# Experts' weights of a two-layer diffusion backbone in transfers of 2 MB, each filling two neighbouring slots of the weight ring

## The reference, cut to what matters

```python
def _ec_moe(h, router, w_gate, w_up, w_down):          # 16 experts, weights 1024 x 1024, float32
    cap = CAPACITY_FACTOR * n // N_EXPERTS             # 64 latent rows, 32 context rows
    aff = softmax(h @ router)
    g, idx = top_k(swapaxes(aff, 1, 2), cap)
    xs = h[bidx, idx]
    a, u = einsum(xs, w_gate), einsum(xs, w_up)
    y = einsum(silu(a) * u, w_down) * g
    return zeros_like(h).at[bidx, idx].add(y)
```

## Time and profile before

| | us |
|---|---|
| median of the runs | 2219.13 |
| the profiled execution, its time | 2219.71 |
| its span, first to last instruction | 2217.9 |
| PE busy (matmuls) | 1863.0 (84%) |
| VectorE, ScalarE, POOL busy | 569.7, 344.6, 265.2 |
| ring's queue (q1): 65952 packets, 480.28 MB | 54.0% of 16 engines' span |
| POOL's queue (q0): 17488 packets, 48.51 MB | 7.6% of 16 engines' span |
| mean granted TensorE clock | 0.927 |

### The profile page before, as it was taken

The page is one execution under the profiler, slowest core; times in us unless marked ns, Lnnn a source line. Parts: engine busy times, 40 slices in busy tenths (PEclk is TensorE's granted clock), DMA queues, the critical chain, the costliest instruction groups (busy, mean ns, idle before and its releaser), DMA issues.

```text
span 2217.9 us, 31845 instructions
## 1 busy us (share of the span) xinstructions
PE 1863.0 (84%) x13406; PEld 981.0 (44%) x13406; DVE 569.7 (26%) x1239; ACT 344.6 (16%) x751; POOL 265.2 (12%) x376
## 2 busy tenths in 40 slices
PE   5799987899958999999997689879977877777872
PEld 2677534586533444444433577457542222222220
DVE  1211136554251111111111221366242101101101
ACT  1110005463220000000000210256220000000001
POOL 1000004300100211211211000140001101101111
PEclk8999997799978999999999899789978999999996
DMA  9224780000237999999998511100136999999995
GB/s 360 89 95 161 286 357 31 1 2 30 105 113 263 384 391 389 397 391 394 393 396 309 231 57 57 57 1 2 59 131 240 398 398 399 402 399 398 405 410 193
DMA packets 86165, 530.88 MB, mean 239 GB/s; under 512 B 11780, under 2 KB 14112, under 8 KB 27424
## 3 DMA queue, kind: packets, MB, share of 16 engines
q1 hardware_dynamic: 65952, 480.28, 54.0%
q0 software_dynamic: 17488, 48.51, 7.6%
q10 hardware_dynamic: 2608, 0.35, 0.1%
HBM read 506.03 MB, written 23.07 MB: 239 GB/s over the span
## 4 chain that ended last, share of the span: by engine, by line
PE 63%; DMA 24%; DVE 7%; ACT 4%; issue 2%; POOL 0%; ACTq 0%; SPq 0%; DVEq 0%; POOLq 0%
DMA ring<-in_w_down 21%; PE psum L1176 14%; PE psum L1179 7%; PE psum L1109 6%; PE psum L886 5%; PE psum L922 5%; PE psum L1006 5%; PE psum L964 5%; PE psum L1061 3%; PE psum L1170 2%; ACT arena L753 2%; PE psum L1032 2%; PE psum L840 2%; DVE smx L1393 2%; DMA ring<-in_w_ada 1%
## 5 line engine op out<-in xcount | busy, mean ns | idle before, releaser
L1170 PE MATMUL psum<-ring,arena 128*64 128x512 f32 x1536 | 376.3, 619 | 103.1 <-DMA ring<-in_w_gate 55.6
L1176 PE MATMUL psum<-ring,arena 128*32 128x512 f32 x3072 | 401.9, 595 | 4.2 <-DVE arena L1531 2.2
L1170 PEld LDWEIGHTS psum<-ring,arena 128*64 128x64 f32 x1536 | 100.4, 139 | 355.9 <-issue 177.2
L1179 PE MATMUL psum<-ring,arena 128*32 128x256 f32 x3072 | 236.5, 380 | 0.0
L1179 PEld LDWEIGHTS psum<-ring,arena 128*32 128x32 f32 x3072 | 99.8, 110 | 230.9 <-issue 230.9
L808 ACT ACTIVATE arena<-psum 128x768 f32<-128x768 f32 (+1 forms) x32 | 22.5, 704 | 1004.7 <-PE psum L1179 516.3
L753 ACT ACTIVATE arena<-psum,smx 128x768 f32<-128x768 f32 (+4 forms) x160 | 119.6, 750 | 239.7 <-DVE smx L1393 239.6
L1006 PE MATMUL psum<-arena 64*128 64x256 f32 (+3 forms) x640 | 121.3, 504 | 40.0 <-ACT arena L753 38.5
L1393 DVE TENSOR_REDUCE smx<-psum 128x1 f32<-128x768 f32 (+4 forms) x160 | 120.7, 761 | 109.0 <-PE psum L1006 56.1
L551 POOL TENSOR_SCALAR arena<-arena,smx 128x768 f32<-128x768 f32 (+1 forms) x40 | 77.9, 1947 | 528.6 <-DVE smx L1421 528.5
L1552 DVE SCALAR_TENSOR_TENSOR arena<-psum,gcur,arena 128x512 f32<-128x512 f32 x32 | 24.0, 751 | 455.0 <-PE psum L1179 229.1
(11 more groups left out here) (224 smaller groups left out, 1604.2 us busy)
## 6 DMA issues: line engine op xcount, KB each, us to landing
ring<-in_w_gate SPq DMA_DIRECT2D x128, 1024.0 KB, 25.9
ring<-in_w_up SPq DMA_DIRECT2D x128, 1024.0 KB, 26.9
ring<-in_w_down SPq DMA_DIRECT2D x128, 1024.0 KB, 28.4
ring<-in_w_ada SPq DMA_DIRECT2D x48, 1024.0 KB, 6.4
ring<-in_w_in SPq DMA_DIRECT2D x18, 1024.0 KB, 21.6
ring<-in_w_out SPq DMA_DIRECT2D x8, 1024.0 KB, 8.2
arena<-residual POOLq DMA_DIRECT2D x14, 512.0 KB, 6.2
residual<-arena POOLq DMA_DIRECT2D x10, 512.0 KB, 2.9
```

What stands on the lines that cost most here:

```text
L1170: ins = mm(psum[64 * n:64 * n + 64, b * 512:(b + 1) * 512], lhs(k), w[:, n * 512:(n + 1) * 512], start=k == 0, stop=k == KD - 1)
L1176: ins = mm(psum[r0:r0 + 32, b * 512:(b + 1) * 512], lhs(k)[:, 32 * g:32 * g + 32], w[:, n * 512:(n + 1) * 512], start=k == 0, stop=k == KD ...
L1179: ins = mm(psum[32 * j:32 * j + 32, (b + 1) * 512:(b + 1) * 512 + 256], lhs_c(k), w[:, j * 256:(j + 1) * 256], start=k == 0, stop=k == KD - 1)
```

## The change

The transfers of the experts' weights are joined in pairs: 2 MB for two neighbouring slots. The three weight tensors are laid out on the host in blocks of 4 x 128 rows and not 2 x 128, so that the 16 KB of a partition are one run in memory (and, as slots are neighbours, one run in the ring). `load_matrix` issues two transfers for each matrix and not four, each after a wait for the second of its slots, with the completion on the semaphore of the first slot alone. PE waits at every second quarter, on that semaphore. So that pairs start at an even slot, an empty unit ("gap") is put ahead of the experts where the number of units is odd, which is so in both layers; PE raises `free` for it after the logits and SP passes over it. `landing` holds the counts to wait for, as slots no longer get equally many transfers. w_out keeps its layout, and so do w_in and w_ada.

```diff
--- before.py
+++ after.py
@@ -238,17 +238,31 @@
             plan(("winC", l, tile), win_all[6 + tile:7 + tile])
         plan_ada(len(rest))
         plan(("wout", l), wout_units(l))
+        if len(units) % 2:
+            plan(("gap", l), [None])
         plan(("exp", l), [None] * (UNITS_E * NE))
 
     free = sem("ring_free")
     landed = [sem(f"ring_landed{s}") for s in range(RING)]
 
+    transfers = [0] * RING
+    landing = {}
+    for n, unit in enumerate(units):
+        if unit:
+            transfers[n % RING] += 1
+            landing[n] = 16 * transfers[n % RING]
+        for l in range(DEPTH):
+            if n == where[("exp", l)]:
+                for m in range(0, UNITS_E, 2):
+                    landing[(l, m)] = 16 * (transfers[(n + m) % RING] + 1)
+                    transfers[(n + m) % RING] += NE
+
     def slot(n, k):
         return ring[:, n % RING, :].rearrange("p (k m) -> p k m", k=k)
 
     def arrive(e, n):
 
-        e.wait_ge(landed[n % RING], 16 * (n // RING + 1))
+        e.wait_ge(landed[n % RING], landing[n])
 
     s_const = sem("const_made")
     s_cload = sem("const_loaded")
@@ -467,6 +481,8 @@
         def load(n):
             if n >= RING:
                 sp.wait_ge(free, n - RING + 1)
+            if units[n] is None:
+                return
             src, k = units[n]
             sp.dma_start(slot(n, k), src).then_inc(landed[n % RING], 16)
 
@@ -483,11 +499,12 @@
             wv = [w[l] for w in (w_gate, w_up, w_down)]
 
             def load_matrix(which, expert, e, m0):
-                for q in range(4):
-                    m = base + m0 + q
-                    sp.wait_ge(free, unit_no(l, e, m0 + q) + (1 - RING))
-                    src = wv[which][expert, q] if isinstance(expert, int) else wv[which][bass.ds(expert, 1), q]
-                    sp.dma_start(slot(m, 2), src).then_inc(landed[m % RING], 16)
+                for q in range(0, 4, 2):
+                    s = (base + m0 + q) % RING
+                    sp.wait_ge(free, unit_no(l, e, m0 + q + 1) + (1 - RING))
+                    src = wv[which][expert, q // 2] if isinstance(expert, int) else wv[which][bass.ds(expert, 1), q // 2]
+                    sp.dma_start(ring[:, s:s + 2, :].rearrange("p u (k m) -> p (u k) m", k=2), src
+                                 ).then_inc(landed[s], 16)
 
             load_matrix(0, 0, 0, GATE0)
             for e, _ in body_experts(sp):
@@ -1131,6 +1148,8 @@
                         ins = mm(bank(6, NE, t * NE), o_h[t % 2][:, k, :], rout[:, l, k, :], start=k == 0, stop=k == KD - 1)
                     ins.then_inc(L["lg"], 1)
 
+            if ("gap", l) in where:
+                pe.sem_inc(free, 1)
             NR = NE if last else 48
             pe.wait_ge(*L("aff", 1))
             for b in range(NX):
@@ -1161,7 +1180,9 @@
                     if q == 2 and between:
                         between(e)
                     m = base + m0 + q
-                    pe.wait_ge(landed[m % RING], e * 16 + 16 * (m // RING + 1))
+                    if q % 2 == 0:
+                        lap, first = divmod(m0 + q, UNITS_E)
+                        pe.wait_ge(landed[m % RING], e * 16 + (landing[(l, first)] + 16 * lap))
                     for kk in range(2):
                         k = 2 * q + kk
                         w = slot(m, 2)[:, kk, :]
@@ -1585,8 +1606,9 @@
 
     nc = bacc.Bacc("TRN2", target_bir_lowering=False, num_devices=1)
     arrays = {f"in_{n}": np.ascontiguousarray(inputs[n]) for n in _INS}
-    for n in ("w_gate", "w_up", "w_down", "w_out"):
-        arrays[f"in_{n}"] = by_partition(inputs[n], 2)
+    for n in ("w_gate", "w_up", "w_down"):
+        arrays[f"in_{n}"] = by_partition(inputs[n], 4)
+    arrays["in_w_out"] = by_partition(inputs["w_out"], 2)
     arrays["in_w_ada"] = by_partition(inputs["w_ada"], 4, 512)
     arrays["in_w_in"] = by_partition(inputs["w_in"], 8, 256)[:, :, 0]
     shape = inputs["x"].shape
```

## The result

The changed kernel takes 2225.62 us (median of 17 runs, 2220.66 to 2232.49) beside 2221.59 for the kernel before (17 runs, 2217.19 to 2225.09): ratio 1.0027, 95% interval 1.0018 to 1.0036, slower by 4 to 8 us, 6 in the middle. Forecast were 2242 us, 23 more than the 2219.1 of before, in a range of 2212 to 2264. The sign, the place and the mechanism were right; the size was four times too large.

The account below looks back on a forecast made before the run. The prediction took PE to set layer 0 and DMA layer 1. Layer 0 +24.5 and layer 1 -1.3 made 2217.9 + 23.2 + 1.8 - 0.6 = 2242.3 us, range 2212 to 2264.

Parts of the forecast that it names:

- part 4: Layer 0: POOL's scatter-gather chain alternates packets with the ring; 25 longer turns add 7.8 to 12.2 us against 6.4 cover.
- The upper bound is that the whole waiting doubles, and I take 3.5: Layer 0's POOL chain: at most +12.2 us; less 6.4 cover the gather is 1.4 to 5.8 us late, 3.5 taken.
- 7 x 3.5 = +24.5: Layer 0's cost in us: seven late gathers at 3.5 us each, within 10 to 41.
- (A): Rival: layer 0's gather stays on time; 2213 to 2228 us, likeliest 2220; chance 0.28.
- (D): Rival: ring runs are still cut to 8 KB, so no packet is saved and no turn grows; 2227 us; chance 0.05.
- the signs that were named: Layer 0: second scatter lands in 14 us or more, gather 12 or more; PE waits 3 to 4 us every second expert.
- Every second expert pays: Layer 0: a late gather gives the next one room, so of 13 gathers 7 pay the lateness.
- The clock's 0 to +10 in layer 0: PE's clock may drop after stalls in layer 0, 1.4 us for each stall; 0 to +10 us, taken 0.
- part 1c: Layer 0: pairs restart DMA one unit later and PE wants second halves sooner; 0 to +5 us, +2 or hidden.
- Layer 1, -1.3: Layer 1's sum in us: pairs cost +2.2 at the start and +1.9 at the end, longer runs give -5.4.
- (C): Rival: 16 KB ring packets are slow as such, 0.96 us for 0.62; about 2750 us; chance 0.03.
- (B): Rival: longer runs gain their full size with the gather on time, layer 1 -5.9, layer 0 0; 2213 us; chance 0.10.

Follow-up runs that it names:

- e5: Kernel before with expert weight runs cut to 4 KB, still 1 MB transfers for one slot; ratio 1.0080.
- e6: One step beyond the change: 4 MB transfers for four slots, 32 KB runs, one PE wait a matrix; ratio 1.0363 against the kernel before.
- e4: Kernel before with four extra POOL operations put ahead of each gather in layer 0's loop; ratio 1.0101.
- a0: The changed kernel measured again, nothing altered; ratio 1.0019 against the kernel before.
- a1: The changed kernel measured a third time, nothing altered; ratio 1.0032 against the kernel before.
- e1: The change's 2 MB transfers for two slots, but with the weight layout and 8 KB runs of before; ratio 1.0025 against the kernel before.
- e9: Changed kernel with the next gather issued earlier in layer 0 alone, and single units at layer 1's start and end; ratio 1.0000 against the kernel before.
- e2: Changed kernel with POOL issuing the next gather right behind the scatters, before they have landed; ratio 1.0018 against the kernel before.
- e2b: The same kernel as e2, measured again; ratio 1.0005 against the kernel before.
- e7: e2 with single 1 MB units for layer 1's first transfers after the start and its last matrix; ratio 1.0001 against the kernel before.

## Why the prediction was right and wrong

**Turns by packet (part 4): right, at its lower bound.** 25 turns of 0.31 us were to lengthen the chain by 7.8 us; it grew by 7.4. The packet counts inside scatters are one for one at 4 KB (e5), 8 KB and 16 KB (after). The second scatter lands after 9.5 us (958.06 to 967.52 in e5's timeline of POOL), 11.4 and 16.3: steps of 1.9 and 4.9 us, where the count of its 18 turns gives 2.7 and 5.6, so the count is near but a little high. At 32 KB (e6, 21.9 and a median of 18.5, where it gives 28) it is far too high, with a ring that isn't always busy there.

**"The upper bound is that the whole waiting doubles, and I take 3.5": the step that failed.** The 12.2 us between a loaded and an unloaded chain were taken as turns that could all double. The turns are only part of it, and the packets of POOL's queue show the other part. A gather's first row starts 1.7 us after its issue when the ring is quiet (issue at 670.77), and 4.1 us after it when the ring is busy, before (971.03) and after (946.90) alike; the scatters' first row starts 0.3 us after the second one's issue when the ring is quiet (1212.70), and 2.9 us after it when it is busy, before and after alike. So 2.4 + 2.6 = 5.0 of the 12.2 us come ahead of the first row and don't grow with the packet, and only the other 7.2 could double. Why a busy ring delays the first row stays open. The lateness was 7.4 - 6.4 = 1.0 us by the landings, 1.2 us by the waits (7.2 in 6 places), where the middle of 1.4 and 5.8 had been taken. The lower bound had been counted packet by packet in a trace row; the upper was a difference of two totals with no mechanism for its remainder. The term 7 x 3.5 = +24.5 should have been +7 to +10; with it the sum gives +6 to +9, 2225 to 2228 us, beside the +6 measured.

**The time alone would not have told.** 2225.6 us lies in the range, but also within the bounds of (A), 2213 to 2228, and beside (D)'s 2227; it is the waits of PE and the packet counts that pick the case. Of the signs that were named, the scatter's landing (14 us or more) and the waits at every second expert came; the gather's landing (12 or more) just missed with 11.5, and the waits were 1.2 us each and not 3 to 4.

**Every second expert pays: right.** 6, 7 and 6 waits in three executions of the change, 8 in e4, where 13 experts could have paid.

**The clock's 0 to +10 in layer 0, taken 0: small for the change, not 0.** In after the granted clock fell to the lower level once that it didn't before, near the layer's end; before has 1.00 at the same place (1198.0 to 1201.4 us):

```profile
1204.50:1207.90 3.40, 3.12 (x20) 0.97 (x24) 0.40 (x2) 0.00 (x0) 0.18 (x1) 0.50 0.53 208
```

3.4 us at half speed cost 1.7 us. With it layer 0 adds up within half a us: waits of 7.2 us for rows, 1.7 of clock, less the 0.9 us of waits for the ring that before had, are 8.0 (measured 7.5); in a0 6.0 + 1.7 - 0.9 = 6.8 (6.7), in a1, with two such stretches, 8.8 + 3.4 - 0.9 = 11.3 (10.8), in e1 3.3 + 1.7 - 0.9 = 4.1 (4.0), and e4 as above. e6 lost 11 us beyond its waits. The stretch between the layers is another matter. It took 476 to 477 us or 480 us, the latter in after, a1 and e9 (and 481 in e6). The windows at 1300 to 1500 us, first before, then after, show PE's granted clock at 0.91 and at 0.88 of full speed:

```profile
1300.00:1500.00 200.00, 175.87 (x856) 119.51 (x856) 75.56 (x147) 56.36 (x121) 35.25 (x16) 0.91 0.11 37
```

```profile
1300.00:1500.00 200.00, 178.14 (x798) 120.99 (x798) 69.81 (x134) 51.56 (x111) 31.85 (x15) 0.88 0.10 37
```

The difference sits about 234 us behind the end of layer 0. There PE's granted clock rose again before, and stayed at the lower level after:

```profile
1443.20:1456.80 13.60, 10.20 (x78) 6.21 (x77) 9.56 (x17) 8.17 (x16) 6.29 (x3) 1.00 0.00 1
```

```profile
1450.30:1463.90 13.60, 12.52 (x64) 7.93 (x60) 6.77 (x13) 6.33 (x13) 5.39 (x3) 0.50 0.01 1
```

Over the whole stretch between the layers the lower level adds up to 122.9 us before and 129.7 after, and 6.8 us at half speed are the 3.4 us. All four long executions have 129.7 us or more, all ten short ones 122.9 or less. The change touches nothing there. Two of its three profiled executions have the longer form, none of the four of kernels with transfers of 1 MB; what picks it stays open. It may be what spreads the change's runs wider (12 us against 8), which is not shown, and it was in no rival.

**Pairs in layer 0 (part 1c), +2 or hidden: right, a little low.** Hidden in the change; once nothing lay over it, 2.8 to 4.2 us of waits in e2 and e2b, and a layer 0 that is 2.4 to 4.0 us longer than before in e2, e2b and e1.

**Layer 1, -1.3: right within its spread.** Measured +0.6, -1.4 and -4.3 in three executions, so one execution tells little here. e1 has the cost side alone at +4.3 (forecast +4.1 less the completions), e7 and e9 the gain side at -5.3 and -4.0 (forecast -5.4). The prediction's rows gave a packet a fixed part of 0 to 14 ns, and half was taken; layer 1's +11.6 us in e5 is 180 units of 8 more packets for each engine, 8 ns a packet.

**Rivals.** (A), the gather on time, fails on the waits of PE. (C) fails on 0.616 us a packet, (D) on the packet count. So the instruction fetches' 0.96 us was no price of a 16 KB ring packet. (B) needs the gather on time and fails with (A); its gain in layer 1 stands by itself in e7 and e9, 4 to 5 us, and their layer 0 eats it.

**The rules weighed.** Round-robin at packet granularity (the Trainium skill, DMA: Bandwidth & Descriptors, Queues, rings and completion order) agrees with the counts at 4, 8 and 16 KB; one run of one partition behaved here as the unit of a turn, where the page speaks of 9 to 17 descriptors. The rule of the Trainium skill, DMA: Bandwidth & Descriptors, Bandwidth, that larger transfers have a better rate, does not show here between 1 and 2 MB: with runs of 8 KB both go at 402 GB/s (before and e1). It is the run that counts, 396, 402 and 407 GB/s at 4, 8 and 16 KB, in steps of little over 1%, and the neighbours pay for it.

## What to carry to other kernels

Before making a transfer's contiguous runs longer, look who else uses the DMA engines in small pieces with somebody waiting: each of its packets waits for one of yours, so its latency grows by about the number of its packets per engine times the growth of yours (7.4 us for a count of 7.8 here, from 8 to 16 KB), and the question is whether the cover exceeds that. Count such a term packet by packet and take the counted bound; a difference of two totals is no range until the trace shows which part of it can grow. Where a loop waits for something issued two rounds earlier, a lateness is paid every second time.

## What the runs showed of the hardware

The ring's queue and POOL's take turns one packet for one, a packet being a partition's whole run, at 4 KB (254 to 242 in e5), 8 KB and 16 KB (265 to 237 in after). The median from the second scatter's issue to its landing went from 11.3 to 16.4 us with 16 KB runs and stayed at 11.7 with 2 MB transfers of 8 KB runs (e1). Under ring traffic a gather's first row starts 4.1 us after its issue at runs of 8 and of 16 KB, and 1.7 us after it without. That clearing away one cause (the late gathers) let another, smaller one (the ring's lead) come forth was expected; that the same kernel's layer 1 differs by up to 5 us between executions (490.5, 493.4, 495.4) was not.
